# Strassen MLP: the third weight sum in the other matmul's buffer, sums and steps of VectorE in other places

## The reference, cut to what matters

```python
m = silu(cond) @ ada_w[layer] + ada_b[layer]      # six modulation vectors
...
h = rmsnorm(x, norm_g[layer, 1]) * (1 + sc2) + sh2
x = x + g2 * (jnp.square(jax.nn.relu(h @ mlp_w1[layer])) @ mlp_w2[layer])
```

## Time and profile before

| | |
|---|---|
| median of 3 runs | 1562.29 us (1562.01, 1562.29, 1566.15) |
| profiled execution, own time | 1565.44 us |
| its span | 1563.6 us |
| mean granted clock of TensorE | 0.995 |
| PE / DVE / ACT / POOL busy | 1521.5 / 1141.8 / 684.8 / 621.9 us |
| matmul instructions on PE | 11754 |

### The profile page before, as it was taken

How to read it: one execution, slowest core, us unless ns; L and a number is a source line. 1 busy time by engine, 2 the same in 40 slices (tenths; PEclk the granted TensorE clock), 3 DMA queues, 4 the chain that set the end, 5 groups by cost and what they waited for, 6 DMA issues and landing times.

```text
span 1563.6 us, 28369 instructions
## 1 busy us (share of the span) xinstructions
PE 1521.5 (97%) x11754; PEld 1480.2 (95%) x11754; DVE 1141.8 (73%) x1877; ACT 684.8 (44%) x1140; POOL 621.9 (40%) x410
## 2 busy tenths in 40 slices
PE   8999999999999999999999999999999999999998
PEld 7999999999999999999998999999999999999998
DVE  5348678675774687898795888773584798889885
ACT  5323333344432354455444534652443355545553
POOL 0233313314222464675574253101333475467541
PEclk9999999999999999999999999999999999999999
DMA  9454333313243234533525122001222212231222
GB/s 328 157 184 147 120 113 120 102 55 108 82 147 117 90 120 148 165 105 122 176 89 167 35 70 73 28 1 55 82 68 68 82 55 82 82 108 55 82 82 82
DMA packets 123168, 162.20 MB, mean 104 GB/s; under 512 B 4640, under 2 KB 87584, under 8 KB 123040
## 3 DMA queue, kind: packets, MB, share of 16 engines
q1 hardware_dynamic: 121808, 159.34, 31.7%
q10 hardware_dynamic: 1232, 1.05, 0.2%
HBM read 156.44 MB, written 3.93 MB: 103 GB/s over the span
## 4 chain that ended last, share of the span: by engine, by line
PE 70%; DVE 15%; ACT 7%; issue 3%; DMA 2%; POOL 2%; SPq 0%; DVEq 0%; ACTq 0%
PE ps L741 41%; PE ps L1165 17%; PE ps L860 2%; DVE fx L2591 2%; DVE raw L2549 2%; PE ps L1413 2%; POOL wL L2028 2%; DVE xT L2600 1%; ACT wH L1475 1%; ACT fx L1799 1%; DMA raw_high<-in_mlp_w 1%; PE ps L1361 1%; DVE ps L2103 1%; PE ps L997 1%; DVE fq L2582 1%
## 5 line engine op out<-in xcount | busy, mean ns | idle before, releaser
L2028 POOL TENSOR_TENSOR wL<-raw,wH 128x512 fp32r<-128x512 f32 x232 | 371.3, 1625 | 737.3 <-ACT wH L1457 521.4
L1165 PE MATMUL ps<-fx,wH 128*128 128x320 f32 x1120 | 251.0, 312 | 15.3 <-DVE held L2605 8.6
L741 PE MATMUL ps<-hH,wH 128*128 128x320 f32 x704 | 221.1, 314 | 2.0 <-DVE hL L2114 1.3
L741 PE MATMUL ps<-hH,wL 128*128 128x320 f32 x704 | 217.6, 309 | 0.0
L741 PE MATMUL ps<-hL,wH 128*128 128x320 f32 x704 | 217.5, 309 | 0.0
L1165 PEld LDWEIGHTS ps<-fx,wH 128*128 128x128 f32 x1120 | 185.8, 188 | 23.4 <-issue 16.7
L2028 POOL TENSOR_TENSOR wL<-raw_high,wH 128x512 fp32r<-128x512 f32 x100 | 142.0, 1450 | 115.0 <-ACT wH L1457 115.0
L1165 PE MATMUL ps<-fx,wL 128*128 128x320 f32 x560 | 173.0, 309 | 0.0
L741 PE MATMUL ps<-wH,hH 128*128 128x256 f32 x560 | 162.1, 290 | 2.4 <-DVE hL L2114 2.1
L741 PE MATMUL ps<-wL,hH 128*128 128x256 f32 x560 | 158.3, 283 | 0.0
L741 PE MATMUL ps<-wH,hL 128*128 128x256 f32 x560 | 158.3, 283 | 0.0
(11 more groups left out here) (298 smaller groups left out, 3747.4 us busy)
## 6 DMA issues: line engine op xcount, KB each, us to landing
ada<-in_ada_w SPq DMA_DIRECT2D x40, 1024.0 KB, 5.2
raw<-in_mlp_w SPq DMA_DIRECT2D x64, 512.0 KB, 3.8
raw_high<-in_mlp_w SPq DMA_DIRECT2D x64, 512.0 KB, 3.9
raw<-in_even_w_in SPq DMA_DIRECT2D x28, 512.0 KB, 5.7
pre_w<-in_ada_w SPq DMA_DIRECT2D x16, 512.0 KB, 8.9
raw<-in_odd_w_qkv SPq DMA_DIRECT2D x10, 512.0 KB, 3.7
raw<-in_even_w_out SPq DMA_DIRECT2D x8, 512.0 KB, 3.5
raw<-in_odd_w_o SPq DMA_DIRECT2D x6, 512.0 KB, 3.4
```

What stands on the lines that cost most here:

```text
L741: last = nc.tensor.matmul(ps[:, bank, 0:width], a_, b_, start=(k == 0 and p_ == 0), stop=(k == nk - 1 and p_ == 2))
L1165: last = nc.tensor.matmul(ps[:, bank, 0:HALF], a_, b_, start=(opens and k == 0 and p_ == 0), stop=(k == nk - 1 and p_ == 2), skip_group_ch ...
L2028: last = nc.gpsimd.tensor_tensor(wL[:, at % 4, cs], source(key)[:, cs], wH[:, at % 4, cs].bitcast(F32), ALU.subtract)
```

## The change

The four sums are computed in the order T3, T2, T1, T4 (T3 = B22 - B12, T2 = T3 + B11, T1 = B12 - B11). T3 is written into the sum buffer of the other matmul (p's first one into a buffer of its own, `t3_begin`), and the raw block B11 is free after its own low part and T1. SP asks for p's B22 and q's B12 ahead of the modulation block that stood before them, and in cycle 7 for the second modulation block after one load in place of three. ACT's high part of S3 stands behind that of S2. DVE's steps stand in another order. The core of the diff:

```diff
             if key[0] in ("p", "q") and key[2] in (T2, T4):
                 return (t24_first if key[0] == "p" else t24_second)[:]
-            return raw(key[:2] + (B11,) if key[0] in ("p", "q") and key[2] == T3 else key)
+            if key[0] in ("p", "q") and key[2] == T3:
+                return (t24_first if key[0] == "q" else t24_second if key[1] % WINO else t3_begin)[:]
+            return raw(key)
...
+            wait_low(engine, *key)
             if key[0] in ("p", "q") and key[2] == B11:
-                wait_low(engine, key[0], key[1], T3)
-            else:
-                wait_low(engine, *key)
+                wait_source(engine, key[:2] + (T1,))
...
                     load_raw(("p", s, T1), p_block(c, 0, 1))
+                    load_raw(("p", s, B22), p_block(c, 1, 1))
                     ada_block(3 * c)
-                    load_raw(("p", s, B22), p_block(c, 1, 1))
...
                     load_raw(("q", s, B11), q_block(c, 1, 0))
+                    load_raw(("q", s, T1), q_block(c, 1, 1))
                     ada_block(3 * c + 1)
-                    load_raw(("q", s, T1), q_block(c, 1, 1))
...
-                        w2(c, 0, (0, 1))
+                        w2(c, 0, (0,))
+                        if c == CYCLES - 1:
+                            ada_block(3 * c + 1)
+                        w2(c, 0, (1,))
                         w2(c, 1, (0,))
-                        if c:
+                        if 0 < c < PLAIN:
                             ada_block(3 * c + 1)
...
-                        operand_hi(c, S3_)
                         hidden_block(c, F22)
                         split_product("q", s2, T3, g + 12)
                         operand_hi(c, S2_)
+                        operand_hi(c, S3_)
...
+                    if i == T3:
+                        wait_raw(dve, which, s, T1)
+                        wait_raw(dve, which, s, B22)
+                        if which == "q":
+                            wait_low(dve, "p", WINO * layer_ + n, T4)
+                        elif n:
+                            wait_low(dve, "q", len(W2) * layer_ + n - 1, T4)
+                        out, a, b, op = t3, b22, b12, ALU.subtract
+                    elif i == T2:
                         wait_raw(dve, which, s, B11)
                         dve.wait_ge(done, 4 * s + 1)
+                        if which == "q":
+                            wait_low(dve, "p", WINO * layer_ + n, T3)
+                        elif n:
+                            wait_low(dve, "q", len(W2) * layer_ + n - 1, T3)
+                        out, a, b, op = t2, t3, b11, ALU.add
+                    elif i == T1:
+                        out, a, b, op = b12, b12, b11, ALU.subtract
...
                     t_lo(s, T1)
+                    modulate(c, 0)
                     t_lo(s, B22)
                     p_add(s, T4)
-                    modulate(c, 0)
                     t_lo(s, B21)
-                    q_add(s2, T1)
                     t_lo(s, T4)
                     combine(c, F11, 0)
+                    q_add(s2, T3)
                     combine(c, F11, 1)
...
-                    q_add(s2, T3)
+                    q_add(s2, T1)
...
                     q_add(s2, T4)
-                    operand_lo(c, S3_)
                     operand_sum(c, S2_)
                     operand_sum(c, S1_)
                     operand_lo(c, S2_)
-                    for m in range(4):
-                        product_out(c, 0, m)
+                    product_out(c, 0, 0)
+                    product_out(c, 0, 1)
+                    operand_lo(c, S3_)
+                    product_out(c, 0, 2)
+                    product_out(c, 0, 3)
...
+                    for m in range(4):
+                        product_out(c, 4, m)
+                    operand_lo(c, A12_)
+                    modulate(c, 2)
+                    p_add(s + 1, T3)
+                    product_out(c, 5, 0)
+                    product_out(c, 5, 1)
+                    p_add(s + 1, T2)
+                    product_out(c, 5, 2)
+                    product_out(c, 5, 3)
+                    product_out(c, 6, 0)
                     p_add(s + 1, T1)
-                    product_out(c, 4, 0)
-                    operand_lo(c, A12_)
...
```

More of the change, by code:

```diff
@@ L87 @@
 Q_ORDER = (B11, T2, T3, T4, T1, B22, B21)
-P_DVE = (T1, B22, B21, T4)
+P_DVE, SUM_ORDER = (T1, B22, B21, T4), (T3, T2, T1, T4)
 BLOCKS, RAW_SEQ = [], []
@@ L158 @@
 F_GROUP = [{F_AT(c, half, k): (k, half) for half in range(2) for k in range(4)} for c in range(CYCLES)]
-A11_, S3_, S2_, A22_, S1_, S4_, A12_ = range(7)
-X_ORDER = (A11_, S2_, S3_, A22_, S1_, S4_, A12_)
+A11_, S2_, S3_, A22_, S1_, S4_, A12_ = range(7)
 F11, F21, F22, F12 = range(4)
@@ L354, in hybrid_step @@
         s_raw = {1: s1_raw, 2: s2_raw, 3: s3_raw, 4: s4_raw}
+        t3_begin = nc.alloc_sbuf_tensor_at("t3_begin", [P, 1024], F32, offset=norm_buffers)
         held = nc.alloc_sbuf_tensor_at("held", [P, KC, HALF], F32, offset=norm_buffers)
@@ L511, in wait_raw_free @@
         def wait_raw_free(engine, key):
+            wait_low(engine, *key)
             if key[0] in ("p", "q") and key[2] == B11:
-                wait_low(engine, key[0], key[1], T3)
-            else:
-                wait_low(engine, *key)
+                wait_source(engine, key[:2] + (T1,))
         def wait_source(engine, key):
             if key[0] in ("p", "q") and key[2] in (T1, T2, T3, T4):
-                engine.wait_ge(p_sum if key[0] == "p" else q_sum, 4 * key[1] + (T1, T2, T3, T4).index(key[2]) + 1)
+                engine.wait_ge(p_sum if key[0] == "p" else q_sum, 4 * key[1] + SUM_ORDER.index(key[2]) + 1)
             else:
@@ L1212, in one @@
                 def one(i, name, bank, m, opens=True):
-                    x = fx[:, (7 * s + X_ORDER.index(name)) % 3]
+                    x = fx[:, (7 * s + name) % 3]
                     block_product(("q", s, i), 512, 2, bank, m, lambda k: [x[:, 0, k, :], x[:, 1, k, :]], opens)
@@ L1788, in operand_hi @@
                     s2 = len(W2) * layer + c - PLAIN
-                    at = X_ORDER.index(name)
-                    if at > 2:
-                        act.wait_ge(acc_full, g0 + G_CYCLE[c] + 14 + 4 * (at - 2))
+                    if name > 2:
+                        act.wait_ge(acc_full, g0 + G_CYCLE[c] + 14 + 4 * (name - 2))
                     if name in (S3_, S2_, S1_, S4_):
@@ L1798, in operand_hi @@
                         src = fq[:, b]
-                    nc.scalar.activation(fx[:, (7 * s2 + at) % 3, 0], src, ACT.Copy).then_inc(x_high, 1)
+                    nc.scalar.activation(fx[:, (7 * s2 + name) % 3, 0], src, ACT.Copy).then_inc(x_high, 1)
                 def hidden_last(b, ms):
@@ L2531, in add_blocks @@
                     b11, b12, b22, b21 = (raw((which, s, n)) for n in (B11, T1, B22, B21))
-                    t24, done = (t24_first, p_sum) if which == "p" else (t24_second, q_sum)
-                    if i == T1:
+                    t2, t3 = source((which, s, T2)), source((which, s, T3))
+                    layer_, n = divmod(s, WINO if which == "p" else len(W2))
+                    done = p_sum if which == "p" else q_sum
+                    if i == T3:
[7 more added lines that the diff above has]
+                    elif i == T2:
                         wait_raw(dve, which, s, B11)
[L2535 to L2538, removed]
                         dve.wait_ge(done, 4 * s + 1)
[L2540 to L2544, removed]
+                        if which == "q":
[5 more added lines that the diff above has]
+                        out, a, b, op = b12, b12, b11, ALU.subtract
                     else:
@@ L2547, in add_blocks @@
                         wait_low(dve, which, s, T2)
-                        out, a, b = t24[:], b21, t24[:]
-                    nc.vector.tensor_tensor(out, a, b, ALU.subtract).then_inc(done, 1)
+                        out, a, b, op = t2, b21, t2, ALU.subtract
+                    nc.vector.tensor_tensor(out, a, b, op).then_inc(done, 1)
                 def q_add(s2, i):
@@ L2588, in operand_lo @@
                            A12_: fq[:, F12]}[name]
-                    x = fx[:, (7 * s2 + X_ORDER.index(name)) % 3]
+                    x = fx[:, (7 * s2 + name) % 3]
                     dve.wait_ge(x_high, 7 * s2 + name + 1)
@@ L2657, in strassen_cycle @@
                         product_out(c, 3, m)
-                    p_add(s + 1, T1)
-                    product_out(c, 4, 0)
-                    operand_lo(c, A12_)
[L2661 to L2667, removed]
+                    for m in range(4):
[9 more added lines that the diff above has]
+                    product_out(c, 6, 0)
+                    p_add(s + 1, T1)
                     for m in range(1, 4):
-                        product_out(c, 5, m)
-                    for m in range(4):
                         product_out(c, 6, m)
@@ L2676, in last_cycle @@
                     s = WINO * layer + c - PLAIN
```

(16 more changed lines are left out.)

## The result

The changed kernel takes 1557.21 us (five runs, 1556.72 to 1557.33), the kernel before 1566.15 us (five runs, 1562.01 to 1566.79). The ratio is 0.9944, with a 95% interval of 0.9931 to 0.9957: faster by 0.56%, beyond the 0.3% that a measurement can tell. The forecast was 1570, slower. The time lies within the stated range and almost on the first rival, "VectorE wins at A22 in every cycle" (1557.5).

The account below looks back on a forecast made before the run. TensorE, busy 97% of the span, was taken as the bound, so only its waits and clock could move. From 1565.44 us: -8.1 for the queue, +8.4 for layer 0, +5.05 for layer 1, rounded to 1570; overall range 1552 to 1574.

Parts of the forecast that it names:

- VectorE wins at A22 in every cycle: First rival: A22's low part gets its turn before POOL's next piece, +0.66 us a cycle; about 1557.5 us, chance 0.22.
- Step 3: S3's low part moved earlier: A22's low part then loses its turn to POOL, +1.92 us in each of ten cycles.
- Step 1: Load queue in layer 0: blocks asked for earlier remove PE waits and a low-clock stretch, -8.1 us.
- Step 2: Seam p to q on DVE: +0.28 us a cycle in layer 1 (ends 0 and 0.34), -0.24 in layer 0.
- Step 4: Seam q to next p: PE's two waits at B22 in layer 1 go, 1.19 us a cycle; moved sums cost nothing.
- Won: Rival: DVE gets the turn at A22's low part in every cycle; about 1557.5 us, chance 0.22.
- Mixed: Rival: A22's turn is won in layer 0 and lost in layer 1; 1564.5 us, no difference, chance 0.15.
- no new wait: Rival: S3's low part does not hold up POOL's piece, so the step fits; 1550.2 us, chance 0.15.
- the fourth rival: Modulation block still late in layer 0's last cycle, 3.2 to 6.1 us come back; 1573 to 1576, chance 0.05.

Follow-up runs that it names:

- three writes: Three small writes to a 128x3 tile on VectorE ahead of A22's low part, against the changed kernel: 1568.41 us (eight runs).

## Why the prediction was wrong, point by point

- **Step 3 failed at one sentence**: "0.03 lies on the losing side. I take lost, in all ten cycles." The turn was won in all ten cycles, and A22's low part took 0.81 in place of 1.97. The walk up to there holds to 0.01, and both branches have now been measured: 1557.2 with the turns won (forecast of that branch 1557.5) and 1568.4 with them lost (forecast 1570). Wrong was how the margin was read. I held DVE's request against the end of POOL's running piece and took two rows as the bounds. POOL's next piece, read beside them, shows that neither is one:

```profile
1212.14 1.29 POOL L2028 TENSOR_TENSOR wL<-raw_high,wH 128x512 fp32r<-128x512 f32 x1
1217.48 2.52 POOL L2028 TENSOR_TENSOR wL<-raw,wH 128x512 fp32r<-128x512 f32 x1
```

  At 1217.38 DVE won without a rival: POOL's next piece, at 1217.48, had waited for ScalarE's high part until 1217.41. At 1212.14 POOL began 0.01 ahead of the DVE step that lost, which is 0.04 ahead of its own running piece's end. At A22 the same 0.04 puts POOL's next piece at E+2.94 and DVE's step at E+2.95, within the walk's own error of each other. The Trainium skill's rule ("SBUF — State Buffer", "Who interferes with whom": whoever issues first gets the shared pair for the whole instruction) made it a tie and was set aside for the row at 1212.15. The runs agree with the rule as far as the whole instruction goes (1.97 against 0.81); which of the two issued first can't be read from rows so close. What they show is that DVE wins about 0.24 ahead of POOL (all ten cycles of the kernel before) and loses 0.02 to 0.03 behind it (all ten with three writes). Within about 0.01 of each other both outcomes occur, and what decides there stays open. A reading that kept to the walk's error would have given the two branches the same chance.
- **Step 1's sum was about right, one clause was not.** The queue alone gave 7.2 of the 8.1, with two new waits of 0.7 idle (1.0 with the 0.16 each). The 0.50 clock went with the wait, and a fall came back with it in the kernel with the old queue. (The 2.9 for the clock should have been 2.8, 6.16 - 3.4.) But "has, by its landing, a stage to spare" is wrong of the modulation block itself, which now has q's B12 ahead of it: 1.8 of idle in the changed kernel, between none and 1.6 in the others that ask in this order.
- **Step 2's numbers were right, the one for layer 1 by luck.** q T2's idle grew by 0.25 in layer 1 (0.28 forecast); in layer 0 the loss of T2 fell by 0.21 to 0.24 (0.24). But with S3's move undone the idle in layer 1 is 1.44 to 1.49: the new order of the sums costs 0.46 to 0.49 there, above the step's upper end of 0.34, and S3's move gives back 0.21 to 0.24, which the prediction counted in layer 0 alone.
- **Step 4 was right**: both waits of q B22 are gone in all five cycles of layer 1, 1.19 each, and p T2 came in time.
- **The rivals.** "Won" is what happened. "Mixed" and "no new wait" did not occur: the small losses at q T3 and T4 (0.14 and 0.40) are there in all ten cycles. The sum of "no new wait" also left out step 2's 0.28 (five times, 1.4). The last cycle's modulation block came in time, so that the fourth rival did not occur either, though blocks came late in two other cycles.
- **The nearness of 1557.2 to "won" (1557.5) is partly luck.** The two new waits for modulation blocks, 2.2 with the 0.16 each, stood in no sum. Against them the cycles cost less than that branch had: in layer 0 one without such a wait grew by 0.04 (T2 to T2, 54.62 to 54.66) and not by 0.42, in layer 1 one shrank by 0.47 (52.00 to 51.53) and not by 0.25. Five times each, that is 3.0.
- **The account, by runs.** The queue alone brings 1564.8 to 1557.6 (-7.2). The rest of the change without S3's move brings that to 1552.0 (-5.6, of which q B22's waits are 6.0, against a longer q T2). S3's move takes 5.1 of it back, to 1557.1. So the change gained little more than its queue's order because one part of it undid another, and not because of the turn, which was won.

## What to carry to other kernels

Where two engines take turns at a resource, walk the schedule with turns, as here, and then look for places where two requests begin within the walk's error of each other: each is a coin with a price, to be stated as such, and best moved apart in the kernel (0.24 us was enough here). The largest gain sat in front of the turn, 9 us with two outputs ahead of S2's low part: steps that take no turn belong into the time in which the other engine holds it, and an in-order load queue wants the block that is needed first ahead of the one that waits for something.

## What was not expected of the hardware

- A delay of 0.01 us at one VectorE instruction of each Strassen cycle changed the time of the program by 8.7 us (1557.05 to 1565.71), since it flipped a turn worth 1.14 us in up to ten cycles; at the edge the runs of one program lie 5.6 us apart, and 0.01 to 0.02 further on 1.9.
- A write of a 128x1 tile is drawn 0.06 us long but moved the instruction behind it by about 0.01.
